# One matmul loop in two: all 512-column matmuls of a weight unit, then all its 256-column ones

## The chip, the cores and the metric

The kernel runs on one core of a Trainium2 chip. The metric is the device time of one execution in microseconds (us). Lower is better. Several runs are taken and the median is compared.

## What is computed

The reference is a stack of three small transformer-like blocks on a sequence of 256 tokens with 2048 features, in fp32. What matters here is that nearly all of its arithmetic lies in products of the activations with large weight matrices:

```python
def _even_layer(x, norm_g, w_in, ...):
    z = _rmsnorm(x, norm_g) @ w_in                     # 2048 x 7168
    ...
    return jnp.concatenate([ya, yb], axis=-1) @ w_out  # 2048 x 2048

def _odd_layer(x, norm_g, w_in, ...):
    z = _rmsnorm(x, norm_g) @ w_in
    ...
    return (o * jax.nn.silu(gate)) @ w_out
```

A third block follows (a gated delta rule, a Fourier mix, two gates and an MLP of 2048 to 8192 to 2048 features). Between the products stand norms, a short attention, a convolution and the delta rule's small 128x128 and 64x64 matrices.

## The kernel before

**Two terms for each operand.** Each fp32 weight and each fp32 activation is split into an upper part and a lower part. The product is made of three of the four cross terms: upper weights times upper activations, upper weights times lower activations, and lower weights times upper activations.

**Units of weights.** Weights come from memory in units of 512 KB, which are 128 partitions x 1024 columns. UK = 4 blocks of 128 input rows stand side by side, each with UN = 256 output columns. There are four slots (SLOTS) in each of the buffers `raw`, `w_hi` and `w_lo`. The SyncE queue loads `raw`. ScalarE writes `w_hi` (lines 648, 659 and 1173). GpSimd writes `w_lo` (line 620) and raises `lo_done`. TensorE waits for `lo_done` once per unit, and raises `unit_used` with the unit's last matmul, upon which ScalarE and GpSimd may fill the slot again. All 716 units pass through these slots in one fixed order.

**Two kinds of product.** Where the output is wanted with features on partitions, `product` is used (lines 2147 to 2166). For each of a unit's four blocks `k` it issues four matmuls. Two have 512 moving columns (line 2160): a 128x128 piece of the upper weights stands in the array, and the activations' upper and lower part, 256 columns each, pass through in one go. Two have 256 moving columns (line 2163): the lower weights stand in the array, and the upper activations pass through. The two matmuls of each pair go to two different banks of PSUM (`m` is 0 or 1). Where the output is wanted with tokens on partitions, `wide_unit` is used (lines 2202 to 2204): there a piece of the activations stands in the array and 512 weight columns move. Its matmuls all have 512 columns, and three in a row go to the same bank. A third form, `pw_unit` (lines 2303 to 2305), serves one small matrix, and all its matmuls have 256 columns; lines 2303 and 2304 use the same piece of upper weights one after the other, line 2305 a piece of the lower ones. The diff touches `product` alone.

**Parts of a unit.** In the delta-rule stage, the function `fill` lays pieces of `product` between small matrices, half a unit (two of the four `k`) at a time, through the argument `ks`. The four pairs of heads use 56 halves each, 224 in all, which are 112 units. Everywhere else `product` takes a whole unit.

**Waits inside a unit.** `product` takes a function `wait`, called for each `k` ahead of its first matmul. It is given only where a product begins on activations that are still being normalised. There TensorE turns a block of them (line 2124 or 2107), ScalarE writes their upper part, VectorE their lower part (line 1237 or 1253), and TensorE waits for row `k` of `a` or `b` in `nm_lo`. This concerns three groups of four units: the first of `even_w_in`, of `w_in_2` and of the MLP. A fourth use, `cq_ready`, waits at `k` = 0 alone.

Of the kernel before, what the change touches and what calls it, by code (L numbers as in the profile page):

```python
# [26 lines left out]
P = 128  # L27
T = 256
TT = T // P
D = 2048  # L30
DC = D // P
# [15 lines left out]
UK, UN = 4, 256  # L47
# [156 lines left out]
def build(nc, t, out):  # L204
    ctx = ExitStack()
    with ctx:
# [57 lines left out]
        lin_ps = ctx.enter_context(nc.psum_tensor("lin_ps", [P, 4, 512], F32))  # L264
# [1824 lines left out]
        def _(pe):  # L2089
# [57 lines left out]
            def product(u, g, parity, q, n, slot, src, k0, wait, free, ks=range(UK)):  # L2147

                if 0 in ks:
                    if q == 0 and free:  # L2150
                        pe.wait_ge(group_free, g - 1)
                    pe.wait_ge(lo_done, u + 1)
                hi = w_hi[:, slot].rearrange("p (k n) -> p k n", k=UK)
                lo = w_lo[:, slot].rearrange("p (k n) -> p k n", k=UK)
                for k in ks:
                    kk = (k0 + q * UK + k) % DC
                    if wait:
                        wait(q * UK + k)
                    for m in range(2):
                        nc.tensor.matmul(lin_ps[:, 2 * parity + m, :], hi[:, k, m * P:(m + 1) * P],  # L2160
                                         src[:, kk].rearrange("p s n -> p (s n)"), start=(q == 0 and k == 0), stop=False)
                    for m in range(2):
                        last = nc.tensor.matmul(lin_ps[:, 2 * parity + m, 0:T], lo[:, k, m * P:(m + 1) * P], src[:, kk, 0, :],  # L2163
                                                start=False, stop=(q == n - 1 and k == UK - 1))
                if UK - 1 in ks:
                    last.then_inc(unit_used, 1)
# [92 lines left out]
            for g in range(16):  # L2259
                for q in range(4):  # L2260
# [5 lines left out]
                    if g == 1 and q == 3:  # L2266

                        pe.wait_ge(op_dve.sem, op_dve.at("rn"))
                        for s in range(TT):
                            m = nc.tensor.matmul(ps[:, 0, T + s * P:T + (s + 1) * P], recip[:, s:s + 1].broadcast_to([P, P]), ident[:], start=True, stop=True)  # L2270
# [6 lines left out]
            for q in range(TT):  # L2277
                for c in range(8):
                    m = nc.tensor.transpose(ps[:, 2 * q + c // 4, (c % 4) * P:(c % 4 + 1) * P], z[:, Z_AGT + c, q * P:(q + 1) * P], ident[:])
            m.then_inc(ln_pe.sem, 1)  # L2280
            for j in range(8):
                if j == 5:

                    pe.wait_ge(ln_dve.sem, ln_dve.at("n11"))
                    for c in range(8):
                        for q in range(TT):
                            m = nc.tensor.transpose(ps[:, c // 2, (c % 2) * T + q * P:(c % 2) * T + (q + 1) * P],
                                                    scr[:, 2 * q + c // 4, (c % 4) * P:(c % 4 + 1) * P], ident[:])
# [69 lines left out]
            for name, width in (("cq", QL), ("kv", KVW)):  # L2358
                bank = 2 * (OG[name] % 2)
                pe.wait_ge(group_free, OG[name] - 1)  # L2360
                for j in range(8):
# [3 lines left out]
                    lo = w_lo[:, u % SLOTS, 0:2 * width].rearrange("p (k n) -> p k n", k=2)  # L2365
                    for k in range(2):
                        kk = 2 * j + k
                        if name == "cq":
                            h_ready(kk)
                        for q in range(TT):  # L2370
# [4 lines left out]
                            last = nc.tensor.matmul(acc, al, hi[:, k, :], start=False, stop=(kk == DC - 1))  # L2375
                    last.then_inc(unit_used, 1)
                if name == "cq":

                    pe.wait_ge(nm_rs.sem, nm_rs.at("rn1", 1))
                    for q in range(TT):  # L2380
                        m = nc.tensor.matmul(ps[:, 3, q * P:(q + 1) * P], recip[:, q:q + 1].broadcast_to([P, P]), ident[:], start=True, stop=True)
# [9 lines left out]
            for c in range(4):  # L2391
                for q in range(TT):
                    m = nc.tensor.transpose(ps[:, c // 2, (c % 2) * T + q * P:(c % 2) * T + (q + 1) * P], cqn[q][:, c * P:(c + 1) * P], ident[:])
            m.then_inc(od_pe.sem, 1)
            pe.wait_ge(od_dve.sem, od_dve.at("kv1"))
            for c in range(2):
                for q in range(TT):
                    m = nc.tensor.transpose(ps[:, 2, c * T + q * P:c * T + (q + 1) * P], ckvn[q][:, c * P:(c + 1) * P], ident[:])
            m.then_inc(od_pe.sem, 1)
            pe.wait_ge(gt_act.sem, gt_act.at("rows"))  # L2400
            for q in range(TT):
                m = nc.tensor.transpose(ps[:, 3, q * P:(q + 1) * P], ikn[:, q * P:(q + 1) * P], ident[:])
# [153 lines left out]
            for c in range(DC):  # L2556
                m = nc.tensor.matmul(ps[0:64, 0, :], sc_w[:, c].rearrange("p h n -> p (h n)"), a[:, c].rearrange("p s n -> p (s n)"), start=(c == 0), stop=(c == DC - 1))
# [268 lines left out]
```

## Time and profile before

| | |
|---|---|
| three runs | 2213.12, 2213.36 and 2214.79 us, median 2213.36 us |
| profiled execution, first to last instruction | 2211.2 us |
| TensorE matmul busy | 2180.4 us, 99% |
| TensorE weight loads busy | 1872.4 us, 85% |
| GpSimd, VectorE, ScalarE busy | 1713.8, 1068.8 and 1031.7 us |
| matmuls, and weight loads | 12563 each |

The profiled execution has no time of its own besides its span. The median of the runs is 2.2 us above that span. A matmul's row gives its start and its duration. The duration covers the whole way through the array, and the next matmul starts long before it is over, so the duration of a row isn't what the matmul costs. What it costs is the distance from its start to the start of the next one. The text calls this distance the matmul's slot. In the view in order of time, neighbouring instructions of one line are merged, so "x2" is two matmuls and the start is that of the first.

### The profile page before, as it was taken

To read this page: it belongs to the slowest core of one execution; us is meant where nothing else is said; L and a number is where in the kernel's file an instruction comes from. 1 tells how busy PE (TensorE), PEld (TensorE's weight loads), DVE (VectorE), ACT (ScalarE), POOL (GpSimd) and SP (SyncE) were. 2 spreads that over 40 slices of the span, in tenths; PEclk is the share of its full clock that TensorE was granted. 3 is DMA by queue.
4 is the path that set the end of the run, shared out by engine and by line. 5 is a ranking of instruction groups with operands and counts; after the bars stand their busy time and mean duration, and the time that the engine had idled before them with its cause. 6 is when DMAs were issued, how large, how long until landed. Compare 5 with 4: busy or idle time off the path is not lost.

```text
span 2211.2 us, 34201 instructions
## 1 busy us (share of the span) xinstructions
PE 2180.4 (99%) x12563; PEld 1872.4 (85%) x12563; DVE 1068.8 (48%) x1812; ACT 1031.7 (47%) x1438; POOL 1713.8 (78%) x721
## 2 busy tenths in 40 slices
PE   8999999999999999999999999999999999999998
PEld 7888888888888878888888888888888888888887
DVE  5994243115863142557575745316704813821842
ACT  5433455454556554535354644444333333333343
POOL 7888868887666966657575758888888888888886
PEclk9999999999999999999999999999999999999999
DMA  7666545655454755445454546655656666666664
GB/s 233 190 191 190 178 146 167 187 155 180 138 146 139 245 151 146 135 133 163 125 160 125 163 133 190 209 191 181 190 194 190 189 195 192 189 193 191 190 190 153
DMA packets 321441, 383.86 MB, mean 174 GB/s; under 512 B 14655, under 2 KB 255782, under 8 KB 321062
## 3 DMA queue, kind: packets, MB, share of 16 engines
q1 hardware_dynamic: 317237, 377.80, 56.5%
q10 hardware_dynamic: 4080, 4.33, 0.6%
q8 instruction: 88, 1.44, 0.3%
q14 instruction: 36, 0.29, 0.0%
HBM read 379.98 MB, written 2.10 MB: 173 GB/s over the span
## 4 chain that ended last, share of the span: by engine, by line
PE 94%; DVE 1%; issue 1%; POOL 1%; ACT 1%; SPq 1%; DMA 0%; ACTq 0%; POOLq 0%
PE lin_ps L2160 36%; PE lin_ps L2163 18%; PE lin_ps L2202 9%; PE lin_ps L2203 9%; PE lin_ps L2204 9%; POOL w_lo L620 1%; PE ps L2670 1%; PE lin_ps L2373 0%; PE ps L2518 0%; PE lin_ps L2375 0%; PE lin_ps L2374 0%; PE ps L2681 0%; PE ps L2679 0%; PE lin_ps L2441 0%; PE lin_ps L2227 0%
## 5 line engine op out<-in xcount | busy, mean ns | idle before, releaser
L620 POOL TENSOR_TENSOR w_lo<-raw,w_hi 128x1024 fp32r<-128x1024 f32 x716 | 1713.5, 2402 | 481.6 <-ACT w_hi L648 372.1
L2160 PE MATMUL lin_ps<-a,w_hi 128*128 128x512 f32 x2176 | 699.4, 403 | 2.4 <-POOL w_lo L620 1.2
L648 ACT ACTIVATE w_hi<-raw 128x1024 fp32r<-128x1024 f32 x456 | 477.6, 1058 | 470.9 <-PE lin_ps L2163 258.3
L2163 PEld LDWEIGHTS lin_ps<-a,w_lo 128*128 128x128 f32 x2176 | 409.9, 188 | 96.0
L2160 PE MATMUL lin_ps<-b,w_hi 128*128 128x512 f32 x1376 | 433.2, 396 | 0.8 <-DVE z L1505 0.8
L2163 PE MATMUL lin_ps<-a,w_lo 128*128 128x256 f32 x2176 | 429.3, 279 | 0.0
L659 ACT ACTIVATE w_hi<-raw 128x1024 fp32r<-128x1024 f32 x228 | 242.1, 1062 | 384.4 <-PE lin_ps L2163 225.3
L2160 PEld LDWEIGHTS lin_ps<-a,w_hi 128*128 128x128 f32 x2176 | 334.1, 190 | 9.9 <-issue 5.6
L2163 PEld LDWEIGHTS lin_ps<-b,w_lo 128*128 128x128 f32 x1376 | 258.9, 188 | 60.5
L2202 PE MATMUL lin_ps<-w_hi,a 128*128 128x512 f32 x752 | 293.7, 391 | 0.0
L2204 PE MATMUL lin_ps<-w_hi,a 128*128 128x512 f32 x752 | 293.0, 390 | 0.0
L2203 PE MATMUL lin_ps<-w_lo,a 128*128 128x512 f32 x752 | 292.9, 390 | 0.0
L2163 PE MATMUL lin_ps<-b,w_lo 128*128 128x256 f32 x1376 | 270.5, 278 | 0.0
L2160 PEld LDWEIGHTS lin_ps<-b,w_hi 128*128 128x128 f32 x1376 | 209.7, 189 | 1.9 <-DVE z L1505 1.3
L2204 PEld LDWEIGHTS lin_ps<-w_hi,a 128*128 128x128 f32 x752 | 141.2, 188 | 29.6
L2202 PEld LDWEIGHTS lin_ps<-w_hi,a 128*128 128x128 f32 x752 | 141.2, 188 | 28.8
L2203 PEld LDWEIGHTS lin_ps<-w_lo,a 128*128 128x128 f32 x752 | 141.3, 188 | 28.5
L1290 DVE SCALAR_TENSOR_TENSOR x<-lin_ps,nst,x 128x512 f32<-128x512 f32 x24 | 16.9, 747 | 219.6 <-PE lin_ps L2204 219.6
L2066 DVE TENSOR_TENSOR a<-scr,a 128x512 f32 x32 | 91.9, 2873 | 5.3 <-DVE a L2064 1.8
L1395 DVE SCALAR_TENSOR_TENSOR ps<-z,vec,ps 128x254 f32<-128x254 f32 (+28 forms) x232 | 88.4, 464 | 0.0
L2062 DVE SCALAR_TENSOR_TENSOR scr<-scr 128x512 f32<-128x512 f32 x32 | 86.8, 2714 | 1.1
L2064 DVE CAST a<-scr 128x512 f32 x32 | 77.9, 2434 | 5.1 <-DVE scr L2062 5.1
(432 smaller groups left out, 2145.0 us busy)
## 6 DMA issues: line engine op xcount, KB each, us to landing
raw<-in_w_in SPq DMA_DIRECT2D x144, 512.0 KB, 3.7
raw<-in_w_mlp_up SPq DMA_DIRECT2D x128, 512.0 KB, 3.7
raw<-in_w_mlp_down SPq DMA_DIRECT2D x128, 512.0 KB, 3.6
raw<-in_even_w_in SPq DMA_DIRECT2D x112, 512.0 KB, 3.6
raw<-in_odd_w_in SPq DMA_DIRECT2D x40, 512.0 KB, 3.6
raw<-in_even_w_out SPq DMA_DIRECT2D x32, 512.0 KB, 4.2
raw<-in_odd_w_out SPq DMA_DIRECT2D x32, 512.0 KB, 4.8
raw<-in_w_o SPq DMA_DIRECT2D x32, 512.0 KB, 4.2
```

Source lines behind the costliest of these rows:

```text
L620: nc.gpsimd.tensor_tensor(w_lo[:, slot], raw[:, slot], w_hi[:, slot].bitcast(F32), ALU.subtract).then_inc(lo_done, 1)
L648: nc.scalar.activation(w_hi[:, slot], raw[:, slot], ACT.Copy).then_inc(hi_done, 1)
L659: nc.scalar.activation(w_hi[:, slot], raw[:, slot], ACT.Copy).then_inc(hi_done, 1)
L1395: nc.vector.scalar_tensor_tensor(out=acc[c][:, k:T], in0=u[c][:, 0:T - k], scalar=per_channel(w + 8 * (TAPS - 1 - k) + c), in1=acc[c][:, k:T],
L2062: nc.vector.scalar_tensor_tensor(out=tm2, in0=tmp, scalar=0.0, in1=tmp, op0=ALU.max, op1=ALU.mult).then_inc(ml_dve.sem, 1)
L2064: nc.vector.tensor_copy(bb[:, :, 0, :], tm2).then_inc(ml_dve.sem, 1)
L2066: nc.vector.tensor_tensor(bb[:, :, 1, :], tm2, bb[:, :, 0, :].bitcast(F32), ALU.subtract).then_inc(ml_dve.sem, 1)
L2160: nc.tensor.matmul(lin_ps[:, 2 * parity + m, :], hi[:, k, m * P:(m + 1) * P], src[:, kk].rearrange("p s n -> p (s n)"), start=(q == 0 and ...
L2163: last = nc.tensor.matmul(lin_ps[:, 2 * parity + m, 0:T], lo[:, k, m * P:(m + 1) * P], src[:, kk, 0, :], start=False, stop=(q == n - 1 and ...
L2202: nc.tensor.matmul(acc, ah, hi[:, k, :], start=(j == 0 and k == 0), stop=False)
L2203: nc.tensor.matmul(acc, ah, lo[:, k, :], start=False, stop=False)
L2204: last = nc.tensor.matmul(acc, al, hi[:, k, :], start=False, stop=(j == 7 and k == 1))
```

## The change

The loop over `k` in `product` is taken apart into two. The first one waits, where there is a wait, and issues the two 512-column matmuls of each `k`. The second one issues the two 256-column matmuls of each `k`. What each matmul reads and writes stays as it was, and so do the flags of the accumulation, the waits for `group_free` and `lo_done`, and the signal `unit_used` behind the last matmul.

```diff
+                row = lambda k: (k0 + q * UK + k) % DC
                 for k in ks:
-                    kk = (k0 + q * UK + k) % DC
                     if wait:
                         wait(q * UK + k)
                     for m in range(2):
                         nc.tensor.matmul(lin_ps[:, 2 * parity + m, :], hi[:, k, m * P:(m + 1) * P],
-                                         src[:, kk].rearrange("p s n -> p (s n)"), start=(q == 0 and k == 0), stop=False)
+                                         src[:, row(k)].rearrange("p s n -> p (s n)"), start=(q == 0 and k == 0), stop=False)
+                for k in ks:
                     for m in range(2):
-                        last = nc.tensor.matmul(lin_ps[:, 2 * parity + m, 0:T], lo[:, k, m * P:(m + 1) * P], src[:, kk, 0, :],
+                        last = nc.tensor.matmul(lin_ps[:, 2 * parity + m, 0:T], lo[:, k, m * P:(m + 1) * P], src[:, row(k), 0, :],
                                                 start=False, stop=(q == n - 1 and k == UK - 1))
```

The order of TensorE's instructions is shown at two places. The first is the program's opening: behind the transposes of `x` (L2124) stands the first unit of `even_w_in`, then the next transposes. Before:

```order
L2124 MATMUL ps<-ident,x 128x128 x16
L2160 MATMUL lin_ps<-a,w_hi 128x512 x2
L2163 MATMUL lin_ps<-a,w_lo 128x256 x2
L2160 MATMUL lin_ps<-a,w_hi 128x512 x2
L2163 MATMUL lin_ps<-a,w_lo 128x256 x2
L2160 MATMUL lin_ps<-a,w_hi 128x512 x2
L2163 MATMUL lin_ps<-a,w_lo 128x256 x2
L2160 MATMUL lin_ps<-a,w_hi 128x512 x2
L2163 MATMUL lin_ps<-a,w_lo 128x256 x2
L2124 MATMUL ps<-ident,x 128x128 x8
```

The same place in the changed program, where line 2163 has become line 2164:

```order
L2124 MATMUL ps<-ident,x 128x128 x16
L2160 MATMUL lin_ps<-a,w_hi 128x512 x8
L2164 MATMUL lin_ps<-a,w_lo 128x256 x8
L2124 MATMUL ps<-ident,x 128x128 x8
```

The four pairs of each kind have become one run of eight. Only the width changes less often: once in the middle of the unit, and once at its end. The transposes stand where they stood.

The second place is the delta-rule stage, where half a unit lies between the small 64x64 matrices of one solving step (L2670) and those of the next (L2679). Before:

```order
L2670 MATMUL ps<-z 64x64 x8
L2670 MATMUL ps<-scr,z 64x64 x8
L2160 MATMUL lin_ps<-a,w_hi 128x512 x2
L2163 MATMUL lin_ps<-a,w_lo 128x256 x2
L2160 MATMUL lin_ps<-a,w_hi 128x512 x2
L2163 MATMUL lin_ps<-a,w_lo 128x256 x2
L2679 MATMUL ps<-z 64x64 x2
```

The same place in the changed program:

```order
L2671 MATMUL ps<-z 64x64 x8
L2671 MATMUL ps<-scr,z 64x64 x8
L2160 MATMUL lin_ps<-a,w_hi 128x512 x4
L2164 MATMUL lin_ps<-a,w_lo 128x256 x4
L2680 MATMUL ps<-z 64x64 x2
```

Here the runs are four long, and the half unit has one change of width inside it instead of three. The small matrices stand where they stood. The instructions of VectorE, ScalarE and the SyncE queue are the same in both programs, in the same order.

## Rows read from the trace of the kernel before

**Rows 1.** The page: span, busy time by engine, and the chain that ended last.
```profile
span 2211.2 us, 34201 instructions
PE 2180.4 (99%) x12563; PEld 1872.4 (85%) x12563; DVE 1068.8 (48%) x1812; ACT 1031.7 (47%) x1438; POOL 1713.8 (78%) x721
...
PE lin_ps L2160 36%; PE lin_ps L2163 18%; PE lin_ps L2202 9%; PE lin_ps L2203 9%; PE lin_ps L2204 9%; POOL w_lo L620 1%; PE ps L2670 1%; PE lin_ps L2373 0%; PE ps L2518 0%; PE lin_ps L2375 0%; PE lin_ps L2374 0%; PE ps L2681 0%; PE ps L2679 0%; PE lin_ps L2441 0%; PE lin_ps L2227 0%
```

**Rows 2.** The page's costliest groups: the four kinds of matmul that the diff reorders.
```profile
L2160 PE MATMUL lin_ps<-a,w_hi 128*128 128x512 f32 x2176 | 699.4, 403 | 2.4 <-POOL w_lo L620 1.2
...
L2160 PE MATMUL lin_ps<-b,w_hi 128*128 128x512 f32 x1376 | 433.2, 396 | 0.8 <-DVE z L1505 0.8
L2163 PE MATMUL lin_ps<-a,w_lo 128*128 128x256 f32 x2176 | 429.3, 279 | 0.0
...
L2163 PE MATMUL lin_ps<-b,w_lo 128*128 128x256 f32 x1376 | 270.5, 278 | 0.0
```

**Rows 3.** TensorE's waits, whole span: us in total, times, longest.
```profile
PE lin_ps L2247 <- DMA ident<-in_c_ident: 8.4, 1, 8.4
PE ps L2182 <- ACT scr L705: 4.4, 1, 4.4
...
PE lin_ps L2160 <- POOL w_lo L620: 1.2, 4, 0.4
...
PE lin_ps L2160 <- DVE a L1253: 0.9, 1, 0.9
```

**Rows 4.** TensorE in order of time, MLP stage: start, us, instruction.
```profile
1704.28 0.63 PE L2160 MATMUL lin_ps<-b,w_hi 128*128 128x512 f32 x2
1704.75 0.39 PE L2163 MATMUL lin_ps<-b,w_lo 128*128 128x256 f32 x2
1704.98 0.63 PE L2160 MATMUL lin_ps<-b,w_hi 128*128 128x512 f32 x2
...
1748.17 0.63 PE L2160 MATMUL lin_ps<-b,w_hi 128*128 128x512 f32 x2
```

**Rows 5.** The same view of a stretch of 512-column matmuls alone.
```profile
1619.93 0.39 PE L2202 MATMUL lin_ps<-w_hi,a 128*128 128x512 f32 x1
1620.16 0.39 PE L2203 MATMUL lin_ps<-w_lo,a 128*128 128x512 f32 x1
...
1658.01 0.39 PE L2202 MATMUL lin_ps<-w_hi,a 128*128 128x512 f32 x1
```

**Rows 6.** The same view of a stretch of 256-column matmuls alone.
```profile
358.27 0.28 PE L2304 MATMUL lin_ps<-b,w_hi 128*128 128x256 f32 x1
358.39 0.29 PE L2305 MATMUL lin_ps<-b,w_lo 128*128 128x256 f32 x1
...
372.31 0.28 PE L2304 MATMUL lin_ps<-b,w_hi 128*128 128x256 f32 x1
```

**Rows 7.** The same view: 256 to 512 columns after a long stretch.
```profile
372.55 0.40 PE L2202 MATMUL lin_ps<-w_hi,b 128*128 128x512 f32 x1
...
373.94 0.39 PE L2202 MATMUL lin_ps<-w_hi,b 128*128 128x512 f32 x1
```

**Rows 8.** The same view: 256 to 512 after a pair, two places.
```profile
1587.27 0.40 PE L2202 MATMUL lin_ps<-w_hi,a 128*128 128x512 f32 x1
...
1588.65 0.39 PE L2202 MATMUL lin_ps<-w_hi,a 128*128 128x512 f32 x1
...
1763.50 0.40 PE L2202 MATMUL lin_ps<-w_hi,a 128*128 128x512 f32 x1
...
1764.87 0.39 PE L2202 MATMUL lin_ps<-w_hi,a 128*128 128x512 f32 x1
```

**Rows 9.** The same view: first 256-column matmuls after 512; a stretch's beginning.
```profile
346.43 0.28 PE L2303 MATMUL lin_ps<-b,w_hi 128*128 128x256 f32 x1
...
349.18 0.28 PE L2305 MATMUL lin_ps<-b,w_lo 128*128 128x256 f32 x1
...
1497.23 0.62 PE L2160 MATMUL lin_ps<-b,w_hi 128*128 128x512 f32 x2
1497.68 0.40 PE L2163 MATMUL lin_ps<-b,w_lo 128*128 128x256 f32 x2
1497.91 0.63 PE L2160 MATMUL lin_ps<-b,w_hi 128*128 128x512 f32 x2
```

**Rows 10.** Three stretches: busy us and instructions of each engine, clock, DMA.
```profile
core 0: us, PE busy (x) PEld busy (x) DVE busy (x) ACT busy (x) POOL busy (x), PEclk, DMA share, GB/s
...
1704.00:1748.00 44.00, 44.00 (x254) 38.42 (x254) 36.90 (x16) 16.94 (x16) 38.13 (x16) 1.00 0.62 190
1600.00:1650.00 50.00, 50.00 (x222) 41.44 (x221) 2.82 (x4) 19.12 (x18) 44.10 (x19) 1.00 0.60 192
358.00:372.50 14.50, 14.50 (x123) 14.50 (x122) 4.96 (x11) 7.88 (x10) 13.04 (x7) 1.00 0.60 195
```

**Rows 11.** VectorE, then TensorE, in order of time: the program's opening.
```profile
10.66 1.67 DVE L1237 SCALAR_TENSOR_TENSOR a<-ps,vec,a 128x256 fp32r<-128x256 f32 x4 [1.21 <-ACT a L697]
...
13.12 1.66 DVE L1237 SCALAR_TENSOR_TENSOR a<-ps,vec,a 128x256 fp32r<-128x256 f32 x4 [0.20 <-ACT a L697]
...
12.42 1.06 PE L2160 MATMUL lin_ps<-a,w_hi 128*128 128x512 f32 x2
...
16.43 0.70 PE L2160 MATMUL lin_ps<-a,w_hi 128*128 128x512 f32 x2
```

**Rows 12.** MLP stage: GpSimd's group of instructions, then who waited for whom.
```profile
L620 POOL TENSOR_TENSOR w_lo<-raw,w_hi 128x1024 fp32r<-128x1024 f32 x17 | 40.9, 2407 | 6.5 <-ACT w_hi L659 6.5
...
ACT w_hi L659 <- PE lin_ps L2163: 27.6, 16, 1.7
POOL w_lo L620 <- ACT w_hi L659: 6.5, 17, 0.5
```

## The prediction

> **What bounds the kernel now.** I read the page first. TensorE's matmuls fill 2180.4 of 2211.2 us, and the chain that ended last lies on five lines of matmuls: 54% on the two lines that the diff reorders, 27% on the three of `wide_unit` [rows 1]. Next I read TensorE's waits. The long ones are the start of the program (8.4 us) and one norm (4.4 us). Line 2160, behind which the changed loop's waits stand, loses 1.2 us to GpSimd and 0.9 us to VectorE in the whole span [rows 3]. So the end is set by the pace at which matmuls follow each other. Nothing is to be had from another engine unless it comes late.
>
> Pace is read from starts, not from durations, since a 512-column matmul that takes 396 to 403 ns [rows 2] is followed by the next one much earlier. Three stretches give the slots.
>
> - **Mixed, as the loop is now.** From 1704.28 to 1748.17 us the pattern of two 512s and two 256s passes 63 times (the first and last row of 64 that begin a pattern). That is 43.89 / 63 = 0.6967 us for the four [rows 4].
> - **512 columns alone.** From 1619.93 to 1658.01 us there are 168 slots: 38.08 / 168 = 226.7 ns each [rows 5].
> - **256 columns alone.** From 358.27 to 372.31 us there are 117 slots: 14.04 / 117 = 120.0 ns each [rows 6].
>
> All three lie in stretches with a granted clock of 1.00, which is the upper level, 2.4 GHz [rows 10]. Two 512s and two 256s at the pace of the unmixed stretches would take 2 x 226.7 + 2 x 120.0 = 693.4 ns. The mixed pattern takes 696.7 ns. Going from one width to the other and back, which I call a round trip, thus costs **3.3 ns** now.
>
> **The change part by part.**
>
> *What it doesn't do.* No matmul and no weight load goes away. There are 12563 of each [rows 1]; every matmul of the loop has another 128x128 piece of weights, and even lines 2303 and 2304, which use the same piece in turn, each load it: 122 loads for 123 matmuls in that stretch [rows 10]. Columns, banks and flags stay. There is no weight load to be saved.
>
> *What it removes.* The loop runs 2176 + 1376 = 3552 matmuls of each width [rows 2], which are 1776 patterns and as many round trips now: 1776 x 3.33 = **5.9 us** in all. Afterwards 332 whole units and 224 half units have one each. (224 halves hold 4 x 224 = 896 of the 3552, the rest are 2656 / 8 = 332 units.) That makes 556 round trips.
>
> *What one of these costs.* It needn't be 3.3 ns, since the cost is spread over several slots and the pattern now turns back before it is through. The trace shows its parts.
> On the way to 512 columns, the six slots behind the long 256-column stretch take 1.39 us where six steady ones take 1.36, a debt of 30 ns [rows 7]. Behind a single pair they take 1.38 at one place and 1.37 at another, a debt of 20 or 10 ns [rows 8].
> On the way to 256 columns something comes back: the first pair behind steady 512s takes 0.23 us for 0.24, a credit of 10 ns, and the first 23 slots of a 256-column stretch take 2.75 us for 2.76, another 10 ns [rows 9].
> So a round trip R lies between 10 - 20 = -10 ns and 30 - 20 + 10 = +20 ns, the last if only one of the credits is earned. A run of eight lies between the pair and the long stretch, and I take the middle, R = 5 ns: 556 x 5 = 2.8 us.
>
> *Sum of these.* 5.9 - 2.8 = **3.1 us saved**, with the ends 5.9 + 5.6 = 11.5 us saved and 5.9 - 11.1 = 5.2 us lost.
>
> *What it moves: the waits for rows.* Ahead of row `k` = 3 TensorE now does three patterns, 3 x 0.697 = 2.09 us; afterwards three pairs of 512s, 6 x 0.227 = 1.36 us. The row is wanted 0.73 us earlier. In the opening VectorE writes the four rows of the first unit from 10.66 to 12.33 us and TensorE starts on them at 12.42; it writes those of the second unit from 13.12 to 14.78, and TensorE starts on that at 16.43 [rows 11]. All four rows are there before the unit begins. The cover is the unit ahead and the transposes between, and I cost this at nothing. With the cover gone it would be at most 0.73 us in each of three groups, some 2 us. Behind that wait stand only TensorE's own matmuls.
>
> *What it moves: the slots' release.* `unit_used` still comes with the unit's last matmul. In the MLP stage ScalarE waits for it in 16 of 16 units, 1.7 us at most, then GpSimd takes 2.41 us, and TensorE is at 44.00 of 44.00 us busy [rows 10, 12]. A unit takes 4 x 0.697 = 2.79 us, three units lie between the release and the need, 8.4 us, and ScalarE's pass and GpSimd's take less than half of that. The release moves by under 20 ns, so nothing comes late. No DMA is moved, since the SyncE queue's order is the same.
>
> *A rule of the Trainium skill.* The 512s alone take 226.7 ns and the 256s alone 120.0 ns [rows 5, 6], which is 13.3 ns above 512 / 2.4 and 256 / 2.4. The Trainium skill ("TensorE: Matmul & The Clock Gate", Back-to-back issue gap) gives the slot of a warm matmul as N / 2.4 + 2.5 ns, 215.8 and 109.2 ns, whatever stands beside it. By that rule the four would take 650.0 ns in either order and the change would do exactly nothing; the trace is 46.7 ns above it and shows the order to matter a little. The same page (LDWEIGHTS) gives a load as P / 1.2, 106.7 ns here, which leaves a run of 256s a margin of 2.5 ns by its own slot; so it warns against this order more than against the old one.
>
> **The sum against the runs.** The profiled execution would go from 2211.2 to 2208.1 us. The runs' median stands 2.2 us above the profile's span, so **2210.2 us** from 2213.36. Of this kernel the measurement can tell about 0.2% from no change, which is 4.4 us.
>
> **The rivals.**
>
> 1. *The forecast.* The round trips become fewer and somewhat dearer: saved 1 to 4 us, about 2210. Chance 0.37.
> 2. *The 3.3 ns isn't owed to the change of width.* It could come from the two banks in turn, which the unmixed stretches don't have in the same way: `wide_unit` stays in one bank for three matmuls. Then it is paid in any order, the saving is 0, and the time is 2213.4. Against it: at 1497.23 us, behind a `wide_unit`, stand two 512s of the loop, in two banks, and they take 0.45 us together, as steady ones do [rows 9]. The page's rule above would come out here too. Chance 0.15.
> 3. *The boundary costs nothing, or even gives.* More than 4.4 us are saved when R is under 2.7 ns. At -1 ns it is 6.5 us, at -5 ns 8.7 us, at -10 ns 11.5 us, so 2202 to 2209, most likely 2207. For it speaks the debt of only 10 ns at 1763.50 [rows 8] against credits of 20 [rows 9]; against it that the debt behind the long stretch is the largest one, 30 ns [rows 7]. Chance 0.36.
> 4. *Slower: the weight loads become the bound in a run of eight 256s.* A load's record lasts 188 to 192 ns, and in the 256-column stretch the loads' row is busy for 14.50 of 14.50 us, while it has gaps in the mixed one, 38.42 of 44.00 [rows 10]. Two of three matmuls of that stretch load the piece that their neighbour used or will use, from a slot just read; here every load is of fresh weights. If each of the 3552 slots of 256 columns took 123 ns instead of 120, that is +10.7 us, less the 3.1 saved: +7.6, 2221. It decides from (4.4 + 3.1) / 3552 = 2.1 ns per slot, at 122.1 ns. Against it: the third matmul there (line 2305) does load another piece, and no slot of that stretch stands out, 120.0 ns over 117 of them [rows 6]. Chance 0.12.
>
> **How the numbers follow.** The time is that of case 1. Case 1 and 2 are within 0.2%: 0.37 + 0.15 = 0.52. Case 3 is faster, 0.36, and case 4 slower, 0.12. The range goes down to R = -5 ns, 2213.4 - 8.7 = 2204.7, which takes in most of case 3, and up to R = 15 ns, where 2.4 us are lost, 2215.8; I put it at 2204.8 to 2216. It leaves out the far end of case 3 and all of case 4, together 0.2.
>
> **What would show it in the profile after.** The starts inside a run of eight 512s should be 227 ns apart in its last slots and some 232 ns on the mean of the first six; those of the 256s 115 ns in the first pair and 120 ns behind it. The 16 matmuls of a steady unit should take 2.78 us where they take 2.79 now. TensorE should have no new wait on line 2160 in the three groups that begin on rows still being written. The step on R is wrong if the unit takes 2.77 us or less, or more than 2.79. The whole is wrong if the 256s stand 122 ns apart or more, if 512s in two banks stay above 230 ns to the end of the run, or if line 2160 waits for rows.

## The result, and the profile after

| | kernel before | changed kernel |
|---|---|---|
| median of 21 runs | 2214.3 us (2212.5 to 2216.0) | 2217.7 us (2215.7 to 2219.3) |
| profiled execution | 2211.2 us | 2216.7 us |
| a unit of the MLP, from starts | 2786.7 ns | 2793.3 ns |

The changed kernel is slower: the ratio is 1.0015, with a 95% interval of 1.0009 to 1.0021. That is 3.4 us by the medians, where 3.1 us less were forecast. The time lies outside the range that was given.

The page of the changed kernel shows the same shape as [rows 1, 2]. The matmuls fill 99%, and the two lines of the loop are 54% of the chain.

```profile
span 2216.7 us, 34201 instructions
...
PE 2184.8 (99%) x12563; PEld 1881.5 (85%) x12563; DVE 1072.7 (48%) x1812; ACT 1032.7 (47%) x1438; POOL 1715.2 (77%) x721
...
PE lin_ps L2160 36%; PE lin_ps L2164 18%; PE lin_ps L2203 9%; PE lin_ps L2205 9%; PE lin_ps L2204 9%; POOL w_lo L620 1%; PE ps L2671 1%; PE lin_ps L2374 0%; PE ps L2124 0%; PE ps L2519 0%; PE lin_ps L2376 0%; PE lin_ps L2375 0%; PE ps L2682 0%; DMA raw<-in_odd_w_out 0%; DMA x<-in_x 0%
...
L2160 PE MATMUL lin_ps<-a,w_hi 128*128 128x512 f32 x2176 | 581.4, 401 | 2.0 <-DVE a L1253 0.9
...
L2160 PE MATMUL lin_ps<-b,w_hi 128*128 128x512 f32 x1376 | 345.1, 393 | 0.8 <-DVE z L1505 0.8
...
L2164 PE MATMUL lin_ps<-a,w_lo 128*128 128x256 f32 x2176 | 321.1, 282 | 0.0
```

The busy sums of the loop's lines aren't comparable with those of before. Durations overlap by more in a run of eight, and overlap counts once. The means of one matmul hardly differ (401 for 403 ns, 393 for 396).

TensorE's waits, in us in total, times and longest, answer to [rows 3]. Nothing new stands behind line 2160: 0.9 us on VectorE as before, 0.8 on GpSimd where it was 1.2.

```profile
PE lin_ps L2248 <- DMA ident<-in_c_ident: 8.5, 1, 8.5
PE ps L2183 <- ACT scr L705: 4.4, 1, 4.4
...
PE lin_ps L2160 <- DVE a L1253: 0.9, 1, 0.9
...
PE lin_ps L2160 <- POOL w_lo L620: 0.8, 3, 0.3
```

So the loss must lie in the slots. In the view in order of time, a row is now a whole run of eight:

```profile
1682.01 2.00 PE L2160 MATMUL lin_ps<-b,w_hi 128*128 128x512 f32 x8
...
1712.73 2.00 PE L2160 MATMUL lin_ps<-b,w_hi 128*128 128x512 f32 x8
1714.58 1.11 PE L2164 MATMUL lin_ps<-b,w_lo 128*128 128x256 f32 x8
1715.53 2.00 PE L2160 MATMUL lin_ps<-b,w_hi 128*128 128x512 f32 x8
...
1746.25 2.00 PE L2160 MATMUL lin_ps<-b,w_hi 128*128 128x512 f32 x8
```

From 1682.01 to 1746.25 us pass 23 units: 64.24 / 23 = 2.793 us each, where four patterns of [rows 4] take 2.787. Inside the unit that starts at 1712.73, the eight 512s take 1.85 us and the eight 256s 0.95 us. The starts that the trace holds in ns, over five units from there, give 1841 and 952 ns. At the pace of the unmixed stretches [rows 5, 6] they would take 1813 and 960. So a debt of 28 ns is paid at every unit, and 8 ns come back.

**One part of the profile's difference isn't the change's.** The profiles are 5.5 us apart, the medians 3.4. The granted clock in the stretch from 785 to 805 us was 0.74 in this profile. TensorE has been idle just before (4.4 us in one piece, at the norm ahead of `w_in_2`), and the clock is at its lower level, 1.2 GHz, for 10.2 us of this stretch; in the profile of before it was 6.8 us.

```profile
core 0: us, PE busy (x) PEld busy (x) DVE busy (x) ACT busy (x) POOL busy (x), PEclk, DMA share, GB/s
785.00:805.00 20.00, 14.69 (x72) 12.62 (x72) 9.41 (x20) 13.42 (x30) 11.53 (x5) 0.74 0.36 106
```

A second profile of the changed kernel (label r_after, below) had 0.83 there, as the kernel before had (6.8 us at the lower level), and a span of 2213.4 us:

```profile
785.00:805.00 20.00, 15.02 (x79) 13.05 (x80) 10.06 (x23) 14.81 (x31) 11.69 (x6) 0.83 0.45 132
```

### The profile page after: what moved, and what is told of

It is laid out like the page before. It is cut to its first block, busy times and chain, and to the rows that moved or that the text cites. A ratio compares the mean times of both kernels' runs of the same rounds, so it can differ in the third digit from the quotient of the medians.

```text
span 2216.7 us, 34201 instructions
## 1 busy us (share of the span) xinstructions
PE 2184.8 (99%) x12563; PEld 1881.5 (85%) x12563; DVE 1072.7 (48%) x1812; ACT 1032.7 (47%) x1438; POOL 1715.2 (77%) x721
## 4 chain that ended last, share of the span: by engine, by line
PE 93%; DVE 1%; issue 1%; POOL 1%; ACT 1%; DMA 1%; ACTq 0%; POOLq 0%
PE lin_ps L2160 36%; PE lin_ps L2164 18%; PE lin_ps L2203 9%; PE lin_ps L2205 9%; PE lin_ps L2204 9%; POOL w_lo L620 1%; PE ps L2671 1%; PE lin_ps L2374 0%; PE ps L2124 0%; PE ps L2519 0%; PE lin_ps L2376 0%; PE lin_ps L2375 0%; PE ps L2682 0%; DMA raw<-in_odd_w_out 0%; DMA x<-in_x 0%
## 5 line engine op out<-in xcount | busy, mean ns | idle before, releaser
L2160 PE MATMUL lin_ps<-a,w_hi 128*128 128x512 f32 x2176 | 581.4, 401 | 2.0 <-DVE a L1253 0.9
L2160 PEld LDWEIGHTS lin_ps<-a,w_hi 128*128 128x128 f32 x2176 | 385.5, 189 | 70.9 <-issue 5.5
L2160 PE MATMUL lin_ps<-b,w_hi 128*128 128x512 f32 x1376 | 345.1, 393 | 0.8 <-DVE z L1505 0.8
L2164 PEld LDWEIGHTS lin_ps<-a,w_lo 128*128 128x128 f32 x2176 | 312.2, 190 | 32.3
L2164 PE MATMUL lin_ps<-a,w_lo 128*128 128x256 f32 x2176 | 321.1, 282 | 0.0
L2160 PEld LDWEIGHTS lin_ps<-b,w_hi 128*128 128x128 f32 x1376 | 247.6, 189 | 46.1 <-DVE z L1505 1.3
L2164 PEld LDWEIGHTS lin_ps<-b,w_lo 128*128 128x128 f32 x1376 | 187.7, 190 | 13.4
L2164 PE MATMUL lin_ps<-b,w_lo 128*128 128x256 f32 x1376 | 191.8, 282 | 0.0
```

## The experiments

The first theory after the result I call D: a run of 256s that has come to its steady 120 ns leaves a debt of some 27 ns to the 512s behind it, and only some 7 ns come back at the next run of 256s, so a round trip costs 20 ns. In pairs, D says, the run is too short to build that debt up. Its rivals were O (the loss lies in the openings and at the lower clock) and S (a round trip's cost grows evenly with the length of a run).

The diffs below are against the changed kernel, where nothing else is said. A line without a sign stands in both.

**e_four: runs of four.**

```diff
+                for part in (ks[:2], ks[2:]) if len(ks) == UK else (ks,):
+                    for k in part:
...
+                        for m in range(2):
+                            nc.tensor.matmul(lin_ps[:, 2 * parity + m, :], hi[:, k, m * P:(m + 1) * P],
...
+                    for k in part:
+                        for m in range(2):
+                            last = nc.tensor.matmul(lin_ps[:, 2 * parity + m, 0:T], lo[:, k, m * P:(m + 1) * P], src[:, row(k), 0, :],
...
```

> Whole units are done in two halves, each with four 512-column and then four 256-column matmuls (half units as in the changed kernel). Theory D (debt): after a run of 256s that has reached its steady 120 ns, the next six 512s take about 27 ns more in all than steady ones, and only about 8 ns come back at the start of the next 256s, so a round trip costs 19 to 20 ns once the runs are longer than a pair. The changed kernel's own half units, where they lie side by side, show 18.6 ns. Then a whole unit takes 2773 + 2 x 19 = 2811 ns where the kernel before takes 2787 and the changed one 2793.5: 332 x 24 ns = 8 us slower than before, ratio 1.0036. Theory S (the cost of a round trip grows evenly with the length of a run, 3.3 ns at two and 20 at eight, so some 9 at four): 2791 ns, ratio 1.0008. Theory O (what is lost in the changed kernel is lost in the openings and to the clock, not in steady units): between the kernel before and the changed one, ratio 1.0005 to 1.0015.

Measured: ratio 1.0032 (1.0019 to 1.0044), medians 2221.1 and 2214.5. In order of time, the MLP (a row is a run of four 512s):

```profile
1682.26 1.09 PE L2161 MATMUL lin_ps<-b,w_hi 128*128 128x512 f32 x4
...
1748.22 1.09 PE L2161 MATMUL lin_ps<-b,w_hi 128*128 128x512 f32 x4
```

47 runs with their 256s take 65.96 us, 1.4034 us for each, 2806.7 ns a unit, or 16.7 ns a round trip. D gave 2811, S 2791. A third arrangement of the same matmuls is slower than both kernels, and O and S have fallen.

In `w_in_2` the same order has another pace, 23 runs in 32.20 us, 2800.0 ns a unit, and so it has in the 32 units behind 1323.8 us. D has no room for two paces of one order:

```profile
807.80 1.09 PE L2161 MATMUL lin_ps<-a,w_hi 128*128 128x512 f32 x4
...
840.00 1.09 PE L2161 MATMUL lin_ps<-a,w_hi 128*128 128x512 f32 x4
```

**e_one: runs of one.**

```diff
                         nc.tensor.matmul(lin_ps[:, 2 * parity + m, :], hi[:, k, m * P:(m + 1) * P],
...
-                for k in ks:
-                    for m in range(2):
                         last = nc.tensor.matmul(lin_ps[:, 2 * parity + m, 0:T], lo[:, k, m * P:(m + 1) * P], src[:, row(k), 0, :],
...
```

> Widths alternate one by one: a 512, then the 256 of the same block and half, in every unit and half unit, as the 32 matmuls of the two lines 2441 and 2443 already do in the kernel before, where a 512 and a 256 take 351 ns together. Theory D gives no rule for runs of one, but those lines do: four take 702 ns where the pattern of pairs takes 696.7, so a unit takes 2808 ns, 444 x 21 = 9.4 us slower than before, ratio 1.0042. If only the number of changes of width counted, at 3.3 ns for each round trip, it would be 8 of them for 4: 13 ns a unit, 5.9 us, ratio 1.0027. If the order of the widths has no part in it, ratio 1.000.

Measured: ratio 1.0041 (1.0028 to 1.0055), as forecast, but not for the reason given. In the MLP a 512 and a 256 take 30.03 us / 85 = 353.3 ns, 2826.7 ns a unit:

```profile
1681.62 0.40 PE L2160 MATMUL lin_ps<-b,w_hi 128*128 128x512 f32 x1
...
1711.65 0.40 PE L2160 MATMUL lin_ps<-b,w_hi 128*128 128x512 f32 x1
```

In `w_in_2` the same order takes 29.82 / 86 = 346.7 ns, 2773.3 ns a unit. That is exactly the pace of the unmixed stretches, with nothing at all for eight round trips:

```profile
804.11 0.39 PE L2160 MATMUL lin_ps<-a,w_hi 128*128 128x512 f32 x1
804.34 0.27 PE L2162 MATMUL lin_ps<-a,w_lo 128*128 128x256 f32 x1
...
833.93 0.39 PE L2160 MATMUL lin_ps<-a,w_hi 128*128 128x512 f32 x1
```

The same pace stands in the last 55 units of the long stretch of `even_w_in`, and 2826.7 ns in all the other long stretches. So theory D is incomplete. What a change of width costs doesn't follow from the order alone. The five runs may show it too: three took 2221.3 to 2221.7 us and two 2224.9 and 2225.1. The other rhythm in the 55 units of `even_w_in` would make 55 x 53.3 ns = 2.9 us, but only one run, of 2221.7 us, was profiled, so this isn't shown.

**e_snake: every second unit the other way round, runs of sixteen.**

```diff
+                if q % 2 and len(ks) == UK and not wait:
+                    for k in ks:
+                        for m in range(2):
+                            nc.tensor.matmul(lin_ps[:, 2 * parity + m, 0:T], lo[:, k, m * P:(m + 1) * P], src[:, row(k), 0, :],
...
+                    for k in ks:
+                        for m in range(2):
+                            last = nc.tensor.matmul(lin_ps[:, 2 * parity + m, :], hi[:, k, m * P:(m + 1) * P],
...
+                else:
+                    upper()
+                    last = lower()
```

> As the changed kernel, but every second unit of a group does its eight 256s first and its eight 512s last, so runs of equal width join across units to sixteen and there is half a round trip for each whole unit. Theory D: a unit takes 2773 + 10 = 2783 ns on the mean, 10 ns less than in the changed kernel and 3.5 less than before; over some 330 units 3.4 us less than the changed kernel and 1.2 us less than before, ratio to before 0.9995. Theory O: as the changed kernel, ratio 1.0010 to 1.0015. Theory S, with a cost still growing from eight to sixteen: no gain over the changed kernel in steady units.

Measured: ratio 1.0001 (0.9992 to 1.0010), medians 2214.4 and 2214.5. From one unit's 512s to those of the next but one:

```profile
1682.18 1.98 PE L2161 MATMUL lin_ps<-b,w_hi 128*128 128x512 f32 x8
...
1743.42 1.98 PE L2161 MATMUL lin_ps<-b,w_hi 128*128 128x512 f32 x8
```

61.24 us for 22 units, some 2783 ns each, and 2783.3 by the starts in ns (the row at 1682.18 us begins the second of two joined runs of 512s). D gave 2783. Half as many round trips at 20 ns: the loss of the changed kernel is gone, within the interval.

**e_steady: the new order in whole units without waits alone.**

```diff
+                for part in (ks,) if len(ks) == UK and not wait else [(k,) for k in ks]:
```

> The new order only in whole units without a wait for rows; the units of the three openings (12 units) and the 112 units done in halves keep the old order. Theory D: the 320 whole units lose 6.8 ns each, 2.2 us, and the halves' 18 ns per trip fall away, so 1 to 2.5 us over before, ratio 1.0005 to 1.0011. Theory O: nothing is left of the loss, ratio 0.9998 to 1.0002, and the stretch at the lower clock near 790 us is 6.8 us long as before, not 10.2.

Measured: ratio 1.0011 (1.0002 to 1.0020), medians 2216.8 and 2214.5, 2.3 us. The stretch at the lower clock was short, 0.83 over 785 to 805 us, as it was in the second profile of the changed kernel, so its length belongs to neither order. The openings keep the old order here and aren't needed for the loss: 320 units x 6.7 ns = 2.1 us account for what was measured.

This run also gives the price of the half units, which lie between the end of `w_in_2` and the next long stretch of `product`. The way from the last matmul of the one to the first of the other is 475.95 us in the kernel before (839.41 to 1315.36), 476.91 in the changed one (842.98 to 1319.89) and 476.15 here (840.55 to 1316.70), where the halves are in pairs again. The new order costs 0.96 us there, and 0.76 us of it is owed to the 224 halves. The second profiles of both kernels (r_before and r_after) give 475.94 and 476.93 us.

**e_bank: one PSUM bank at a time.** The changed order, with the loops over `m` and `k` exchanged in both halves of the unit:

```diff
+                for m in range(2):
+                    for k in ks:
...
                         nc.tensor.matmul(lin_ps[:, 2 * parity + m, :], hi[:, k, m * P:(m + 1) * P],
...
+                for m in range(2):
+                    for k in ks:
                         last = nc.tensor.matmul(lin_ps[:, 2 * parity + m, 0:T], lo[:, k, m * P:(m + 1) * P], src[:, row(k), 0, :],
...
```

> The changed order, but within each run of eight the four matmuls of one PSUM bank come first and then the four of the other, instead of the two banks in turn. If the two banks in turn cost anything, the steady 512s and 256s get shorter than 227 and 120 ns, or the debt at the change of width gets smaller. My theory says that banks have no part in it: a unit takes 2793 ns as in the changed kernel, and the ratio to before is that of the changed kernel, 1.001 to 1.0015.

Measured: ratio 1.0012 (1.0003 to 1.0022), and in the MLP 64.24 us for 23 units, to the hundredth what the changed kernel takes:

```profile
1682.73 2.00 PE L2160 MATMUL lin_ps<-b,w_hi 128*128 128x512 f32 x8
...
1746.97 2.00 PE L2160 MATMUL lin_ps<-b,w_hi 128*128 128x512 f32 x8
```

Taking the banks in turn has no part in it.

**w384_mixed and w384_grouped: another width.** What they leave as it is and what they add to the computation stands in the first expectation. The line is changed in the kernel before for the one, and in the changed kernel for the other:

```diff
-                        last = nc.tensor.matmul(lin_ps[:, 2 * parity + m, 0:T], lo[:, k, m * P:(m + 1) * P], src[:, kk, 0, :],
+                        last = nc.tensor.matmul(lin_ps[:, 2 * parity + m, 0:384], lo[:, k, m * P:(m + 1) * P], src[:, kk].rearrange("p s n -> p (s n)")[:, 0:384],
```

> The order of the kernel before (pairs), but the lower weights' matmuls are 384 columns wide instead of 256: they also multiply the lower weights by the lower part of half of the tokens, a small term that the reference's split leaves out. Every slot of these should be 160 + 13.3 = 173.3 ns, so the kernel takes 3552 x 53.3 = 189 us more than before, about 2403 us. Theory L (the debt of a change of width is owed to the 256s being so short that a weight load hardly fits beside them; 173 ns leave room): the pattern of four takes 800 ns, a unit 3200, with nothing for the round trips. Theory W (any change of width costs, whatever the widths): 803 ns, a unit 3213, as before.

> The order of the changed kernel, with the lower weights' matmuls 384 columns wide, as in the run beside it. Theory L: all 512s at 227 ns, all 384s at 173, from the first on; a unit takes 3200 ns, and the two kernels with 384 columns differ by less than 0.05%. Theory W: the first six 512s of a run take about 27 ns more than steady ones as they do behind 256s, and a unit takes 3220, 7 ns above the pairs, so that this kernel is 2 to 3 us slower than the one with pairs, ratio 1.001.

Measured: 2433.1 us in pairs, 2414.6 us in runs of eight. Both theories gave the two within 3 us of each other. They are 18.4 us apart, four runs of each, and the grouped order wins. The MLP in pairs, 48 patterns in 39.68 us, 3306.7 ns a unit:

```profile
1859.82 0.63 PE L2160 MATMUL lin_ps<-b,w_hi 128*128 128x512 f32 x2
...
1899.50 0.63 PE L2160 MATMUL lin_ps<-b,w_hi 128*128 128x512 f32 x2
```

In runs of eight, 19 units in 62.07 us, 3266.8 ns each:

```profile
1859.74 2.01 PE L2160 MATMUL lin_ps<-b,w_hi 128*128 128x512 f32 x8
...
1921.81 2.01 PE L2160 MATMUL lin_ps<-b,w_hi 128*128 128x512 f32 x8
```

Unmixed slots of 226.7 and 173.3 ns would make 3200. Theory L has fallen: with more room beside a weight load the change of width costs more, not less. W has fallen too as it was stated, since the same orders rank the other way round.

**w512_mixed: no change of width.** As w384_mixed, with all 512 columns.

> The order of the kernel before, but the lower weights' matmuls are 512 columns wide as well: they also multiply the lower weights by the lower part of the activations, a term that the reference's split leaves out. The order of reading from the buffers of upper and lower weights, the banks and the waits stay. If it is the change of width that costs (theory W), every slot is 227 ns and a unit takes 16 x 226.7 = 3627 ns, with no slot of 230 to 238 ns in steady units. If it is the change between the two weight buffers, or the two banks, units take 13 to 27 ns more than that. The whole: 3552 x 106.7 = 379 us above before, about 2593 us.

Measured: 2581 us in a single run (2593 was expected). In the MLP, 43 patterns of four in 38.98 us are 226.6 ns a matmul:

```profile
1979.93 0.62 PE L2160 MATMUL lin_ps<-b,w_hi 128*128 128x512 f32 x2
...
2018.91 0.62 PE L2160 MATMUL lin_ps<-b,w_hi 128*128 128x512 f32 x2
```

With one width the order of pairs costs nothing against an unmixed stretch. It still alternates between the buffers of upper and lower weights. So the cost is owed to the mixing of widths, and to neither the buffers nor the banks. Of the 12 us by which the whole missed its expectation, 5.9 are the round trips of the kernel before, which the expectation didn't take off. The rest stays open.

**r_before and r_after: both kernels once more.**

> The kernel before once more, for a second profile: the pattern of four at 696.7 ns again, and near 790 us a stretch at the lower clock, 6.8 us long as in its first profile, if its length belongs to the kernel; 10.2 us, as in the changed kernel's profile, if it depends on when in the run it falls.

> The changed kernel once more, on the chip of the two others: a unit of the MLP at 2793.3 ns, ratio to before 1.001 to 1.002. Near 790 us the stretch at the lower clock is 10.2 us long as in its first profile if its length belongs to the kernel, or 6.8 us if it doesn't.

Measured: the pattern of before takes 44.59 / 64 = 696.7 ns again:

```profile
1703.74 0.63 PE L2160 MATMUL lin_ps<-b,w_hi 128*128 128x512 f32 x2
...
1748.33 0.62 PE L2160 MATMUL lin_ps<-b,w_hi 128*128 128x512 f32 x2
```

The changed kernel takes 2793 ns a unit again, ratio 1.0015 (1.0006 to 1.0024). The stretch at the lower clock is 6.8 us long in both, so the 10.2 us of the first profile don't belong to the changed kernel. The spans of the two second profiles, 2212.7 and 2213.4 us, are only 0.7 us apart, where the first two were 5.5 apart: the comparison of the kernels rests on the medians and the slots, not on single spans.

**e_snake2: as e_snake, with half units and openings in pairs.**

> Every second whole unit of a group does its 256s first, as in the run that joins runs to sixteen (2783.3 ns a unit there against 2786.7 before), and half units and units with a wait for rows keep the old order. With 3.3 ns a unit saved in some 320 units it should be 1.1 us faster than before, ratio 0.9995, which the timing can hardly tell from no change; the profile should show 2783.3 ns for a unit of the MLP.

Measured: ratio 0.9997 (0.9988 to 1.0006), 2783.3 ns a unit. As expected, and not to be told from no change by time.

**e_survey: four orders in the four phases of the MLP.** `pairs` is the order of before and `turns` the alternating one. Phase 3 takes this line:

```diff
+                if v == 3:
+                    return pairs[:4] + turns[4:] if q == 0 else turns
```

> The kernel before, with another order of the sixteen matmuls in each of the four MLP phases, to be read from the profile stretch by stretch; all else is as before. The run with widths alternating one by one showed two paces for the same order, 2773 ns a unit in one stretch and 2827 in others, so the pace depends on how a stretch is entered. Phase 1: the first unit of a group in pairs, the other three alternate. Phase 2: alternate, with the 256 first in all but a group's first unit. Phase 3: as phase 1, but only the first block of a group is in pairs. Phase 4: two 512s, then alternate, then two 256s, in each unit. Theory P (the pace locks to one of a few rhythms, chosen by the last slots before): each phase has a steady mean that is 2773.3 ns plus a multiple of 3.3, in three of them other than 2826.7, and at least one is under the 2786.7 of before. Theory N (what counts is only how often the width changes): phases 1 to 3 at 2820 ns or more, the slowest being phase 2, and phase 4 about the same.

Measured, as means of a unit over the steady groups of each phase: 2816.7, 2821.7, then 2774 and 2824 in turn, and 2820.0 ns. The third phase is the telling one. These rows are the pair at the start of each group of four units:

```profile
1854.04 0.61 PE L2182 MATMUL lin_ps<-b,w_hi 128*128 128x512 f32 x2
...
1865.32 0.63 PE L2182 MATMUL lin_ps<-b,w_hi 128*128 128x512 f32 x2
...
1876.42 0.63 PE L2182 MATMUL lin_ps<-b,w_hi 128*128 128x512 f32 x2
...
1887.71 0.63 PE L2182 MATMUL lin_ps<-b,w_hi 128*128 128x512 f32 x2
```

From 1865.32 to 1876.42 us a group takes 11.10 us, some 2774 ns a unit. The next takes 11.29, some 2824 ns a unit. All groups have the same instructions. The pair turns the rhythm each time it comes, from the slow one to the fast one and back. Theory N has fallen. P was right in that other paces than 2827 came up and that one of them lies below 2786.7, but only every second group of the third phase does.

**e_lock and e_lock2: turn the rhythm once.** All in pairs, except that `w_in_2` and the MLP alternate (`style[0]`), and one block of the MLP's first units is done as a pair, once for each phase. In e_lock `even_w_in` alternates as well.

```diff
+                    flip = style[1] == (q, k) and not paired
+                    if flip:
+                        style[1] = None
+                    steps = [(p, m) for p in (1, 0) for m in range(2)] if paired or flip else [(p, m) for m in range(2) for p in (1, 0)]
...
+                style[:] = ["turns", (0, 2)]
                 linear(UNIT0["mlp"] + 64 * ph, GROUP0["mlp"] + 12 * ph, 8, 4, b, waits=turned_in(3) if ph == 0 else None)
+                style[0] = "pairs"
```

> Widths alternate one by one in 57 units of the first matrix and their neighbours, in the 16 of w_in_2, and in the MLP, where the third block of the first unit of each phase (in phase 1: of the second group) is done as a pair, which in the survey's third phase turned the slow rhythm into the fast one; all the rest is in pairs as before. Theory P (an order has more than one rhythm, and the slots before decide which): these units take 2773.3 ns, the pace of the unmixed stretches, 13.3 ns less than before, in about 200 units: 2.7 us faster than before, ratio 0.9988. If the pair set once doesn't turn the rhythm, the MLP's units take 2827 ns as in the run that alternates everywhere, and with 124 of them the kernel is 3 to 4 us slower than before, ratio 1.0015.

Measured for e_lock: all four phases of the MLP at 2773.3 ns a unit, and `w_in_2` as well, but `even_w_in` at 2826.7 in the same 55 units in which e_one had 2773.3. Ratio 0.9997 (0.9988 to 1.0006). The lock held where no stall comes between. In `even_w_in` TensorE waits for VectorE near the start, which made a slot of 0.50 us in e_one and of 0.54 in e_lock. The rhythm changed across this stall in both, and not the same way: the slots ahead of it were those of the slow rhythm in e_one and of the fast one in e_lock, and behind it those of the other. Whether the stall's length or the rhythm ahead of it decides isn't shown.

> As the run before, but even_w_in is in pairs again: its alternating stretch ran at 2773 ns a unit in one profile and at 2836 in another, after a stall of another length ahead of it, so it can't be relied on. What stays is w_in_2 (14 units in one stretch) and 124 units of the MLP at 2773.3 ns for 2786.7: 138 x 13.3 = 1.8 us faster than before, ratio 0.9992, with all four phases of the MLP at 2773.3 ns a unit again. Had the fast rhythm been chance, one phase or more would be at 2827 ns.

Measured for e_lock2: ratio 0.9991 (0.9982 to 1.0000), medians 2212.2 and 2214.4. All four phases are at 2773.3 ns a unit again. The pair that turns the rhythm, in the MLP's second phase:

```profile
1677.03 0.40 PE L2168 MATMUL lin_ps<-b,w_hi 128*128 128x512 f32 x1
1677.27 0.28 PE L2171 MATMUL lin_ps<-b,w_lo 128*128 128x256 f32 x1
1677.38 0.63 PE L2168 MATMUL lin_ps<-b,w_hi 128*128 128x512 f32 x2
1677.85 0.39 PE L2171 MATMUL lin_ps<-b,w_lo 128*128 128x256 f32 x2
1678.08 0.40 PE L2168 MATMUL lin_ps<-b,w_hi 128*128 128x512 f32 x1
```

And behind it, 87 slots of a 512 and a 256 in 30.16 us, 346.7 ns each:

```profile
1703.73 0.40 PE L2168 MATMUL lin_ps<-b,w_hi 128*128 128x512 f32 x1
...
1733.89 0.39 PE L2168 MATMUL lin_ps<-b,w_hi 128*128 128x512 f32 x1
```

This is the fastest of the kernels tried, 2.2 us under before by the medians, where the changed one is 3.4 above it. The upper end of its interval touches 1, so that it beats the kernel before rests on the slots more than on the timing.

## Why the prediction was wrong

- **What bounds the kernel: right.** TensorE's slots set the end before and after, and no other engine came into it.
- **No load, column or wait saved: right.** There are 12563 matmuls in both, and line 2160's waits are the same within half a us.
- **The slots of unmixed runs: right.** Eight 256s in a row settle at 120 ns and eight 512s at 227 ns, in two banks as in one (e_bank). With this the slower rival (weight loads become the bound, 122 ns or more) is out, though the sign was its sign. The rival on the banks is out too, by e_bank and w512_mixed.
- **The step that failed: "A run of eight lies between the pair and the long stretch, and I take the middle, R = 5 ns."** Measured: 2793.3 - 2773.3 = 20.0 ns in each unit. That was the upper end of my own bounds, reached as that end said, with the debt of the long stretch and one credit only: 1841 ns for 1813 are 28 ns of debt, 952 for 960 are 8 ns of credit. Behind a run of eight, the debt is already that of the stretch of 120 in [rows 7], whose six slots are 28 ns too long by the starts in ns. The second credit didn't exist here: the 256s of the changed kernel take 113, 119 and then 120 ns each. A unit of more than 2.79 us is what the prediction itself had named as the sign that R was wrong.
- **The signs and the sum didn't agree.** The prediction expected 232 ns on the mean of the first six 512s and 115 ns for the first pair of 256s. That is a debt of 6 x 5.3 = 32 ns and a credit of 10, so R = 22 ns and a unit of 2.795 us, where the sum took 5 ns and gave 2.78. The signs came true (231 and 116 ns). Had the sum been made from them, it would have come out slower.
- **There was no middle to take.** The prediction read the debts behind a single pair [rows 8] as 20 and 10 ns from starts with two decimals. In ns they are 27 and 10. So one of the two places already had the debt of the long stretch, 28 ns, after a run of two, and a run's length doesn't set it. Pairs are cheap for another reason: over fourteen units of the kernel before, a round trip pays 13 ns on its two 512s and gets 10 back on its two 256s. A run of eight pays 28 and gets back 8.
- **The sum with R as measured:** 332 whole units lose 20.0 - 4 x 3.33 = 6.7 ns each, 2.2 us. The halves lose 0.76 us (e_steady). Together that is 3.0 of the 3.4 us, and the interval is 2.0 to 4.7 us. The prediction gave every one of the 556 round trips one price. With 20 ns for all it would have been 5.2 us lost: by the same count a half unit's round trip costs 2 x 3.33 + 3.4 = 10 ns on the mean, half of a whole unit's.
- **The rule set beside the trace:** The Trainium skill ("TensorE: Matmul & The Clock Gate", Back-to-back issue gap) gives N / 2.4 + 2.5 ns as the gap of an isolated matmul, and says that in a stream with weight loads both operations set the spacing. The prediction's "whatever stands beside it" says more than the page does. By the formula nothing would change. The trace disagrees: the same matmuls in five orders took 2773.3 to 2826.7 ns a unit. The margin of 2.5 ns, and the warning that the prediction drew from it, were worked out from two figures of the page and don't stand on it. They weren't borne out as a mechanism, since the 256s kept 120 ns.
- **The chances:** I gave "slower by over 0.2%" 0.12 and "within 0.2%" 0.52. The ratio, 1.0015, lies within 0.2%, but on the side that my time denied.

Beyond that, the idea of one price for a change of width was too simple. The runs show rhythms: e_one and e_four run at two paces with one order, and in e_survey the same group alternates between them. What stays open is what makes the rhythm, and so why eight is dearer than two. The causes that I could name (too little room beside a weight load, the banks, the buffers) were tried and fell.

## What to carry to other kernels

Where matmuls of two widths follow each other, their order moved TensorE's pace by up to 1.9% here with 512 and 256 columns, with nothing else changed. With 512 and 384 two orders were 1.2% apart, and they stood 2.1 and 3.3% above the unmixed slots. The cost isn't proportional to how often the width changes: runs of two were better than four and eight, and eight better than two at 384 columns. So read the starts over a hundred matmuls in a steady stretch for each order that is cheap to try, rather than reason from columns. Where a price is bounded by rows at both ends, ask which row resembles the new state, not which number lies in the middle: here the run of eight had come to the steady slot of the long stretch, and the long stretch's debt was the price. And where a price is some 10 ns, starts with two decimals are too coarse to tell it from one place.

## What the runs showed of the hardware that I had not expected

A unit here is eight 512s and eight 256s, by starts in steady stretches at a granted clock of 1.00:

| order | ns a unit |
|---|---|
| alternating, fast rhythm (e_one in `w_in_2` and `even_w_in`, e_lock and e_lock2 in `w_in_2` and the MLP) | 2773.3 |
| runs of sixteen (e_snake, e_snake2) | 2783.3 |
| pairs (before) | 2786.7 |
| runs of eight (changed kernel, e_bank) | 2793.3 |
| runs of four, one rhythm (e_four in `w_in_2` and in 32 units behind 1323.8 us) | 2800.0 |
| runs of four, the other (e_four elsewhere) | 2806.7 |
| alternating, slow rhythm (e_one in the MLP, e_lock in `even_w_in`) | 2826.7 |

All of them stand a multiple of 3.33 ns above the first, and the first is what the unmixed slots make. With 384 in place of 256 columns, pairs stand 107 ns and runs of eight 67 ns above the 3200 of unmixed slots. In the MLP's four phases the fast rhythm followed the one block done as a pair each time, in two kernels (e_lock, e_lock2). The rhythm also changed across a stall, from slow to fast in e_one and from fast to slow in e_lock.
